# Opening of a fused four-layer kernel: GpSimd takes six row tiles of the conditioning products, the first products stand ahead of the norm, and the second weight chunk is split in halves

## The reference

```python
cond = jax.nn.silu(c)                                   # c: 1024 values
mod = (cond @ ada_w[layer] + ada_b[layer])[:, None, :]  # ada_w: 1024 x 6144
sh1, sc1, g1, sh2, sc2, g2 = jnp.split(mod, 6, axis=-1)
u = rms_norm(h, norm_g[layer, 0]) * (1.0 + sc1) + sh1
proj = (u @ w_in).astype(jnp.float32)                   # w_in: 1024 x 4096, float32
```

## Time and profile before

| what | value |
|---|---|
| median of three runs | 2948.37 us |
| the profiled execution | 2947.44 us |
| its span | 2945.7 us |
| PE busy | 2916.8 us, 99% |
| DVE busy | 1498.0 us, 51% |
| ACT busy | 1129.0 us, 38% |
| POOL busy | 30.3 us, 1% |

### The profile page before, as it was taken

One profiled execution on the slowest core, in us unless ns is written; L12 is line 12 of the kernel. 1 busy time (PEld: TensorE's weight loads), 2 busy tenths in 40 slices (PEclk: granted clock), 3 DMA queues, 4 the chain that ended last, 5 costly groups with the idle time before them and its releaser, 6 DMA issues.

```text
span 2945.7 us, 38424 instructions
## 1 busy us (share of the span) xinstructions
PE 2916.8 (99%) x16306; PEld 2406.3 (82%) x16306; DVE 1498.0 (51%) x2142; ACT 1129.0 (38%) x1739; POOL 30.3 (1%) x44
## 2 busy tenths in 40 slices
PE   7999999999999999999999999999999999999999
PEld 6878888887887777888888878888888877888887
DVE  6776654555255566633325755543333654643342
ACT  5555421225233333522225465442233455433231
POOL 0000000000000000000000000000000000000000
PEclk9999999999999999999999999999999999999999
DMA  8443355533332222232323222223222222222332
GB/s 293 169 137 115 115 194 173 183 132 89 98 100 72 72 72 67 85 99 96 99 93 101 84 75 72 90 96 100 92 94 93 87 86 72 86 90 96 100 100 86
DMA packets 223640, 313.57 MB, mean 106 GB/s; under 512 B 16400, under 2 KB 123248, under 8 KB 223472
## 3 DMA queue, kind: packets, MB, share of 16 engines
q1 hardware_dynamic: 207520, 266.96, 28.6%
q0 software_dynamic: 10880, 41.95, 3.9%
q10 hardware_dynamic: 5072, 2.23, 0.3%
HBM read 308.98 MB, written 2.11 MB: 106 GB/s over the span
## 4 chain that ended last, share of the span: by engine, by line
PE 91%; DVE 4%; ACT 2%; DMA 2%; issue 1%; SPq 0%; ACTq 0%; POOLq 0%; DVEq 0%
PE G L2093 47%; PE G L2100 25%; PE G L2135 4%; PE G L2152 4%; PE X L2413 1%; PE X L2197 1%; PE G L2118 1%; DMA ada_raw<-in_ada_w 1%; PE X L2427 1%; PE X L2512 1%; PE X L2522 1%; DVE w_lo L1264 1%; PE G L2469 1%; PE X L2424 1%; DVE acc L1301 0%
## 5 line engine op out<-in xcount | busy, mean ns | idle before, releaser
L2093 PE MATMUL G<-u_hi,w_hi 128*128 128x512 f32 x2096 | 836.1, 399 | 0.0
L2093 PE MATMUL G<-u_hi,w_lo 128*128 128x512 f32 x2096 | 818.1, 390 | 0.0
L2093 PE MATMUL G<-u_lo,w_hi 128*128 128x512 f32 x2096 | 817.3, 390 | 0.0
L1264 DVE TENSOR_TENSOR w_lo<-raw,w_hi 128x2048 fp32r<-128x2048 f32 (+2 forms) x238 | 535.9, 2253 | 521.9 <-ACT w_hi L658 521.0
L658 ACT CAST w_hi<-raw 128x2048 fp32r<-128x2048 f32 (+3 forms) x242 | 455.1, 1881 | 532.4 <-DMA raw<-in_w_ff 246.2
L2093 PEld LDWEIGHTS G<-u_hi,w_hi 128*128 128x128 f32 x2096 | 393.8, 188 | 86.5 <-issue 8.1
L2093 PEld LDWEIGHTS G<-u_hi,w_lo 128*128 128x128 f32 x2096 | 393.5, 188 | 84.4
L2093 PEld LDWEIGHTS G<-u_lo,w_hi 128*128 128x128 f32 x2096 | 394.2, 188 | 78.0 <-issue 1.4
L2100 PE MATMUL G<-w_lo,ff_hi 128*128 128x512 f32 x448 | 174.4, 389 | 0.0
L2100 PE MATMUL G<-w_hi,ff_lo 128*128 128x512 f32 x448 | 174.4, 389 | 0.0
L2100 PE MATMUL G<-w_hi,ff_hi 128*128 128x512 f32 x448 | 174.4, 389 | 0.0
(11 more groups left out here) (454 smaller groups left out, 4125.2 us busy)
## 6 DMA issues: line engine op xcount, KB each, us to landing
raw<-in_w_ff SPq DMA_DIRECT2D x128, 512.0 KB, 4.5
raw<-in_ffn_w_in SPq DMA_DIRECT2D x88, 512.0 KB, 4.6
ada_raw<-in_ada_w POOLq DMA_DIRECT2D x40, 1024.0 KB, 7.1
raw<-in_w_in SPq DMA_DIRECT2D x56, 512.0 KB, 4.4
raw<-in_attn_w_in SPq DMA_DIRECT2D x96, 256.0 KB, 3.8
raw<-in_ffn_w_out SPq DMA_DIRECT2D x40, 512.0 KB, 4.7
raw<-in_hgrn_w_in SPq DMA_DIRECT2D x32, 512.0 KB, 4.6
raw<-in_attn_w_in SPq DMA_DIRECT2D x24, 512.0 KB, 4.7
```

Of the source, the lines that this page charges most:

```text
L1264: tt(w_lo[slot][:, 0:nk, 0:w], raw[slot][:, 0:nk, 0:w], w_hi[slot][:, 0:nk, 0:w].bitcast(F32), ALU.subtract).then_inc(s_lo, 1)
L2093: ins = mm(G[0:c1_ - c0, m, :], w[iw][:, k, c0:c1_], xs[ix][:, x0(b) + kk, :], start=first, stop=last, skip_group_check=True)
```

## The change

Four things are changed, all ahead of the 60th microsecond:

1. GpSimd multiplies and adds the last two row tiles of p = 2 and the last four of p = 3: one multiplication over all of them by a broadcast of `cond`, then additions of halves until one tile is left. It does so ahead of the first `ada_raw` loads in its program. DVE does two products fewer for p = 2 and four fewer for p = 3. `first_sum` of the two adds two accumulators, DVE's and GpSimd's, with eight instructions instead of four.
2. DVE does the first two products of p = 0 ahead of the reciprocal of the norm.
3. ACT casts the first row tile of chunk 0 behind three copies of x instead of ahead of them, and DVE makes its `w_lo` behind `first_x(0)` instead of ahead of `first_add(0)`.
4. ACT casts chunk 1 in two halves, the second behind `u_hi` of tile 4; `first_sum(3)` on PE moves from behind row tile 3 to behind its first output tile.

```diff
@@ gpsimd
+            def first_products(p, done):
+                count = ON_POOL[p]
+                src = first_raw[p][:, 1, 4 - count:4, :]
+                c = cond[:, 8 - count:8].unsqueeze(2).broadcast_to([P, count, 512])
+                pool.wait_ge(s_ada_first[p][1], 16)
+                nc.gpsimd.tensor_tensor(src, src, c, ALU.mult).then_inc(s_pstep, 1)
+                while count > 1:
+                    done, count = done + 1, count // 2
+                    pool.wait_ge(s_pstep, done)
+                    nc.gpsimd.tensor_tensor(src[:, 0:count, :], src[:, 0:count, :], src[:, count:2 * count, :], ALU.add).then_inc(s_pstep, 1)
+
+            pool.wait_ge(st["cond"], 1)
+            first_products(2, 0)
+            first_products(3, POOL_STEPS[2])
@@ scalar
             for k in (3, 2, 0, 1):
                 n.take(st["normed_transposed"])
                 n.give(sc.copy(tmp[:, k, :], X[:, k, :]), st["normed_copied"])
+            for k in range(4, 7):
+                normed(k)
             act.wait_ge(s_raw[0], 32)
             n.give(sc.copy(w_hi[0][:, 0, :], raw[0][:, 0, :]), st["first_k_upper"])
-            for k in range(4, 7):
-                normed(k)
...
                 if k == 3:
-                    first_w(1)
+                    act.wait_ge(s_raw[1], 32)
+                    n.give(sc.copy(w_hi[1][:, 0:2, :], raw[1][:, 0:2, :]), st["first_k_upper"])
+                if k == 4:
+                    sc.copy(w_hi[1][:, 2:4, :], raw[1][:, 2:4, :]).then_inc(s_hi, 1)
@@ vector
+            n.take(st["cond"])
+            first_products(0, range(2, 4))
             n.take(st["std"])
             n.give(v.reciprocal(rstd[:, 1, :], rstd[:, 0, :]), st["rstd"])
-            n.take(st["cond"])
-            first_products(0, range(2, 8))
+            first_products(0, range(4, 8))
             first_products(1, range(2, 8))
-            n.take(st["first_k_upper"])
-            n.give(tt(w_lo[0][:, 0, :], raw[0][:, 0, :], w_hi[0][:, 0, :].bitcast(F32), ALU.subtract), st["first_k_lower"])
...
             first_x(0)
+            n.take(st["first_k_upper"])
+            n.give(tt(w_lo[0][:, 0, :], raw[0][:, 0, :], w_hi[0][:, 0, :].bitcast(F32), ALU.subtract), st["first_k_lower"])
             first_u(0)
...
-            first_products(2, range(6, 8))
-            first_products(3, range(8))
+            first_products(3, range(4))
             first_add(2)
@@ tensor
             def first_sum(p):
                 pe.wait_ge(s_astep, 8 * p + 8)
...
+                accumulators = [first_acc(p)]
+                if p in ON_POOL:
+                    pe.wait_ge(s_pstep, sum(POOL_STEPS[i] for i in ON_POOL if i <= p))
+                    accumulators.append(first_pool_acc(p))
...
+                            if (s, k, m) == (0, 3, 1):
+                                first_sum(3)
                             ins = step(s, m, k)
                     if s == 0:
                         ins.then_inc(s_inner, 1)
-                        first_sum(3)
```

More of the change, by code:

```diff
@@ L282, in build @@
                                              "normed_copied", "mix", "bounds_ready", "first_k_upper", "first_k_lower")}
-        s_astep, s_asum, s_mod = sem("ada_product_added"), sem("ada_summed"), sem("mod_ready")
+        s_pstep, s_astep, s_asum, s_mod = sem("first_ada_product_by_pool"), sem("ada_product_added"), sem("ada_summed"), sem("mod_ready")
         s_dve, s_act = sem("dve_order"), sem("act_order")
@@ L414, in build @@
         FIRST_ADA, FIRST_SUMS = (0, 2, 1, 3), (G[:, 3, 0:256], G[:, 3, 256:512], X[:, 3, 0:256], X[:, 2, 0:256])
-        ON_PE = {0: 2, 1: 2, 2: 2}
+        ON_PE, ON_POOL, POOL_STEPS = {0: 2, 1: 2, 2: 2}, {2: 2, 3: 4}, {2: 2, 3: 3}
         FIRST_COLS = 64
@@ L421, in first_acc, with first_pool_acc @@
             k = ON_PE.get(p, 0)
+            return first_raw[p][:, k // 4, k % 4, :]
+        def first_pool_acc(p):
+            k = 8 - ON_POOL[p]
             return first_raw[p][:, k // 4, k % 4, :]
@@ L841, in _ @@
                 n.give(sc.activation(n_tokens[:, j, :], h[:, j, :], ACT.Identity, scale=rstd[:, 1, j:j + 1]), st["x_normed"])
-            def first_w(s):
-                act.wait_ge(s_raw[s], 32)
-                sc.copy(w_hi[s][:, :, :], raw[s][:, :, :]).then_inc(s_hi, 1)
             for k in (3, 2, 0, 1):
@@ L850, in _ @@
                 n.give(sc.copy(tmp[:, k, :], X[:, k, :]), st["normed_copied"])
-            act.wait_ge(s_raw[0], 32)
-            n.give(sc.copy(w_hi[0][:, 0, :], raw[0][:, 0, :]), st["first_k_upper"])
             def normed(k):
@@ L860, in _ @@
                 normed(k)
+            act.wait_ge(s_raw[0], 32)
+            n.give(sc.copy(w_hi[0][:, 0, :], raw[0][:, 0, :]), st["first_k_upper"])
             n.own(st["normed_copied"])
@@ L1319, in first_products @@
                         ins = stt(first_acc(p), src, c, first_acc(p), ALU.mult, ALU.add)
-                    ins.then_inc(s_astep, 1 + first if k == first else 1)
+                    ins.then_inc(s_astep, 1 + (first if k == first else 0) + (ON_POOL.get(p, 0) if k == 7 - ON_POOL.get(p, 0) else 0))
             def first_add(p):
@@ L1549, in _ @@
             first_u(3)
-            first_products(2, range(6, 8))
-            first_products(3, range(8))
+            first_products(3, range(4))
             first_add(2)
-            dve.wait_ge(s_hi, 2)
+            n.take(st["first_k_upper"])
             n.give(tt(w_lo[1][:, 0:2, :], raw[1][:, 0:2, :], w_hi[1][:, 0:2, :].bitcast(F32), ALU.subtract), st["first_k_lower"])
@@ L1559, in _ @@
             first_u(4)
+            dve.wait_ge(s_hi, 2)
             tt(w_lo[1][:, 2:4, :], raw[1][:, 2:4, :], w_hi[1][:, 2:4, :].bitcast(F32), ALU.subtract).then_inc(s_lo, 1)
@@ L2279, in first_sum @@
                 pe.wait_ge(s_astep, 8 * p + 8)
-                for q in range(4):
-                    ins = mm(FIRST_SUMS[p][:, FIRST_COLS * q:FIRST_COLS * q + FIRST_COLS], first_acc(p)[:, blk(q)], ones[:, 0:FIRST_COLS],
-                             start=p not in ON_PE and q == 0, stop=True, skip_group_check=True)
+                accumulators = [first_acc(p)]
+                if p in ON_POOL:
+                    pe.wait_ge(s_pstep, sum(POOL_STEPS[i] for i in ON_POOL if i <= p))
+                    accumulators.append(first_pool_acc(p))
+                for i, acc in enumerate(accumulators):
+                    for q in range(4):
+                        ins = mm(FIRST_SUMS[p][:, FIRST_COLS * q:FIRST_COLS * q + FIRST_COLS], acc[:, blk(q)], ones[:, 0:FIRST_COLS],
+                                 start=p not in ON_PE and q == i == 0, stop=i == len(accumulators) - 1, skip_group_check=True)
                 ins.then_inc(s_asum, 1)
```

## The result

The changed kernel takes 2952.59 us (median of 22 runs, 2950.45 to 2957.67); the kernel before, run beside it, takes 2947.84 (22 runs, 2945.23 to 2952.81). The ratio is 1.0017, with a 95% interval of 1.001 to 1.0023. So it is slower by some 4.8 us, 0.16%. That is under the 0.2% that I set as the bound of what can be told from no change, but with 22 runs of each the interval lies clear of 1: the slowing is real. The forecast was 2947.5, the same within its noise.

A forecast was written before the change was run, and what follows sets the result against it. The prediction took the microseconds PE loses ahead of its steady stretch, at three places, as the bound. Its sum, 2947.44 - 0.9 (value taken at the chain at 108), gave 2946.5 us profiled, 2947.5 as median; range 2944.8 to 2955.0.

The forecast's parts named there:

- DVE's side is relieved: Products of p = 2 and p = 3: DVE does two and four fewer, done at about 37.3; adds nothing to the gain.
- rival 1: From 28.26 us, DVE and GpSimd shut each other out; 2953 to 2955.5 us, value 2954; chance 0.30.
- the two bounds: GpSimd's time for seven tiles at p = 3: 4.2 us at DVE's subtraction rate, 8.2 at the rate of DVE's scan.
- the chain at 108: PE's 0.77 us wait for DVE at 108.39: change between +1.9 and -2.1 us; value taken, DVE 0.9 earlier.
- Does GpSimd deliver in time?: GpSimd's work for p = 3: starts at 34.4, takes 8.2 us, done at 42.6 to 42.8, needed at 43.0.
- rival 2: GpSimd alone is late: first_sum(3) waits 2 to 4 us, DVE not slowed; 2949 to 2952, value 2950.5; chance 0.13.
- Part 1: Opening: two products ahead of the norm gain 0.25 us, the moved w_lo costs 0.26; first product stays at 27.9.
- Part 2, the sums: first_sum(2) and (3): 0.81 us longer each; row tile 4 at 47.0, no clock fall, first block ends 1.85 earlier.
- Part 3, the cast: Second half behind u_hi of tile 4: costs ACT about 1.0 us; PE waits 0.5 for w_lo at 58.1.
- The first ada_raw loads: Issued at about 43 instead of 36.20, arriving at 50 to 52, still covered by one to two microseconds.
- Rival 3: DVE's loads are no bound at 108, so the whole gain of 2.1 us arrives; 2946.2; chance 0.10.

The follow-up runs named there:

- Experiment 5: experiment 1 plus three GpSimd memsets of 1024 columns at p = 2 and three copies of 2048 at p = 3, results unused; 2951.45 us, single run.
- experiment 7: experiment 4 with first_sum(3) back behind row tile 3; 2946.77 us, ratio 1.0002 to the kernel before.
- experiment 1: The changed kernel without GpSimd's arithmetic: DVE makes all products, sums of four instructions, block 4 loads early; 2943.37 us, ratio 0.9991 to the kernel before.
- experiment 4: experiment 1 with ACT's cast of weight chunk 1 in one piece again; 2943.43 us, ratio 0.999 to the kernel before.
- experiment 8: The changed kernel with the six row tiles computed by neither DVE nor GpSimd, so part of the computation is missing; 2945.22 us, ratio 0.9998 to the kernel before.
- experiment 2: The kernel before with only GpSimd's arithmetic and its longer sums added, first_sum(3) where it was; 2954.40 us, ratio 1.0027 to the kernel before.

## Why the prediction was wrong

- **The step that failed** is "DVE's side is relieved". The sum put GpSimd's work at no cost for DVE: rows of unchanged length, "done with p = 3 at about 37.3". Measured: 45.99, since DVE lost 9.2 us to GpSimd and saved 4.7, so that `first_sum(3)` waited for DVE and not for PE's own place. The arithmetic for this case stood ready in rival 1, to which the prediction gave 0.30: 9.4 us of DVE's work and 6.1 to 11.7 of GpSimd's in a row from 28.26. It came out nearly so, 18.1 us from 27.89 on, with 9.5 for GpSimd. The rows that it weighed said nothing on the question: seven SCALAR_TENSOR_TENSOR unharmed beneath two POOL issues show issues and no arithmetic, as it said itself, and the TENSOR_SCALAR of 0.69 for 0.49 lies over an issue too. Experiment 5 has the like of both, a TENSOR_SCALAR of 0.73 and two-operand instructions unharmed, under memsets, while under copies all are longer. The Trainium skill (SBUF — State Buffer, § Who interferes with whom) has this very distinction, two SBUF inputs against GpSimd's reads and fast modes against GpSimd in general. The runs agree with the first clause (6.90 for 1.53 under reads, 0.67 unchanged under memsets). TENSOR_SCALAR's 0.73 for 0.48 under memsets fits the second, but whether it was blocked for a whole memset these rows don't show.
- **The size of rival 1 was too large.** It priced `first_sum(3)` at 6.4 us late, by the scan's 1.17 us for 512 columns. It came at 46.05 instead of 43.0: 3.05. GpSimd needs 0.90 us for 512 columns in long instructions (3.60 / 4), between the two bounds. That the chain at 108 is late too was right in kind, but not by "6 to 7": `tmp` was 2.58 us later than before. So it was 2952.6, just under the rival's own 2953 to 2955.5. That the measured time lies inside the stated range comes of rival 1 being in it, not of the forecast.
- **Does GpSimd deliver in time?** Its last addition ended at 43.28 (predicted 42.6 to 42.8; "ahead of 43" was missed by a little). For p = 3 it began at 35.22 (predicted 34.4) and its rows hold 7.9 us, some 6.5 of work and 1.4 of waiting for DVE, where I had 8.2 of work and no waiting. So the nearness of the end is partly luck. PE waited for DVE (done at 45.99), not for GpSimd, so rival 2 didn't occur.
- **Part 1**: first product at 27.82 (predicted 27.9). DVE's products of p = 1 wait for their load, the moved `w_lo` takes what is left. Right.
- **Part 2, the sums**: +1.0 us each for four more instructions (predicted 0.81). No fall of the clock, and the stretch behind row tile 4 shorter by 1.5 (predicted 1.4). The number is right, the reason isn't: the 2.19 us of waiting did not shrink to 0.3 but went into 1.54 + 1.12 us of new waits, and row tile 4 came at 50.23, not 47.0. Nor does a wait of 2.19 us bring the fall each time: experiment 7 has the same wait and no fall. So the 1.4 us of clock in the sum need not be there in every execution, and hitting them was luck.
- **Part 3, the cast**: 1.03 us a half (predicted 1.0), and PE's wait for `w_lo` 0.48 (predicted 0.5); `w_lo` and PE both came there some 3 us later than predicted, so the difference held and the places didn't. By experiments 1 and 4 it costs nothing measurable.
- **The first ada_raw loads**: covered, as predicted. DVE took them up at 56.75 without waiting.
- **The chain at 108**: the prediction took a value between two cases, DVE 0.9 us earlier. DVE's `tmp` came 2.58 later, and PE waited 1.24 us there for 0.77. With GpSimd's arithmetic out it came at 104.60 (experiment 1) and 105.27 (experiment 4), 3.8 and 3.1 us earlier than before, so the loads on its way did not hold it at its old place.
- **Rival 3, the whole gain** (2.1 us): with GpSimd's arithmetic out, experiments 1 and 4 reach 2.7 and 2.6 us under the kernel before. So the opening held about what the prediction had counted. By experiment 7 it lies in the early sum together with the order around it, within what these intervals can tell, and by experiment 8 none of it lies in GpSimd's help.

**What stays open.** From `tmp` at 110.97 (2.58 us later) to the end of the span (3.4) another 0.8 us arises in this pair of executions. The profiles show where: PE is 2.56 us later at 168.28 and 3.73 later at 319.84, and between them it waits 1.47 us for a `w_lo` (L2171, at 291.19), a wait that the kernel before doesn't have at that place. Why that `w_lo` is late no run tested. Nor is it known why the medians differ by 4.8 and the profiles by 3.4; the profiled execution was one of the fastest of its kernel. The version to keep is experiment 1 or 4: 2.6 us under the kernel before, at the edge of what 11 runs show.

## What to carry to other kernels

In this kernel GpSimd did not relieve DVE of float32 work with two SBUF operands while DVE was busy with its like: each 512 columns on GpSimd took 0.9 us from DVE, each product moved saved it 0.79, and the additions that join the parts (four of ten tiles here) come on top. Before moving work, list what the other engine does in that stretch by operands read, and ask whether an engine that did the work for nothing would gain anything: experiment 8 says no here. The cheap part of a bundled change may carry its whole gain, as the early sum seems to here; so time the parts apart.

## What the runs showed of the hardware

- The shutting out goes both ways and by whole instructions. With DVE's `w_lo` (27.89 to 29.65) in front, GpSimd's multiplication of 1024 columns ended at 31.40; with that `w_lo` at 28.49 to 30.25 (experiment 2) it ended at 32.00, a row of 2.85 us instead of 2.30. Both end 1.75 us behind DVE's end. Alone that instruction takes 1.89. A GpSimd row's length thus holds its waiting, and the profile doesn't mark it; so it is with the long DVE rows.
- GpSimd's float32 tensor_tensor takes 3.60, 1.89 and 1.06 us for 2048, 1024 and 512 columns; a memset of 2048 takes 1.81. The Trainium skill (GPSIMD Engine Reference, § 3.1) gives 4497 ns for 2048 (an addition). Here it was 3595 alone and 3600 beside DVE (multiplications), and the measurement decides.
- The clock fell behind the wait of 4.89 us in experiment 2 (0.75 from 45 to 52 us, and 3.67 us for the sum that took 2.00). Behind shorter waits it did not behave alike: it fell behind 2.19 us in the kernel before (0.76 from 45 to 52) and stayed up behind 2.19 in experiment 7 (1.00); it stayed up behind 1.54 and 1.12 in the changed kernel, and fell behind 1.39 in the profile of experiment 1 (0.50 from 44 to 46). So one profile doesn't tell what the clock will do behind a wait of this length.
- When the clock first rises differs from one execution to the next: 1.00 from 28 to 35 us in experiment 1, 0.60 before. In the changed kernel an earlier rise would bring PE sooner to its wait of 1.54 us for DVE, so little would be gained by it; no run shows that.
